# Second block's feed-forwards of a two-block network on one Trainium2 core: later gate/up groups and two down groups as pairs of 64-row matmuls, four outputs to a group

## The reference

```python
def swiglu_2(h, w_gate, w_up, w_down):
    return (jax.nn.silu(h @ w_gate) * (h @ w_up)) @ w_down

# in each layer l of second_block:
#   hdn = swiglu_2(rms_norm(x, norm_pre[l, 0]), ffn1_w_gate[l], ffn1_w_up[l], ffn1_w_down[l])
#   x = x + 0.5 * rms_norm(hdn, norm_post[l, 0])
#   ... the mixer of the layer ...
#   hdn = swiglu_2(rms_norm(x, norm_pre[l, 2]), ffn2_w_gate[l], ffn2_w_up[l], ffn2_w_down[l])
#   x = x + 0.5 * rms_norm(hdn, norm_post[l, 2])
```

## Time and profile before

| what | value |
|---|---|
| time, median of 3 runs | 3773.07 us |
| fastest and slowest of the 3 | 3771.24 and 3773.1 us |
| span of the profiled execution, first to last instruction | 3763.7 us |
| median less that span (launch and end of the program) | 9.4 us |
| PE busy | 3619.1 us, 96% |
| DVE busy | 2059.1 us, 55% |
| ACT busy | 1319.3 us, 35% |

### The profile page before, as it was taken

One profiled execution on the slowest core, in us unless ns is written; L12 is line 12 of the kernel. 1 busy time (PEld: TensorE's weight loads), 2 busy tenths in 40 slices (PEclk: granted clock), 3 DMA queues, 4 the chain that ended last, 5 costly groups with the idle time before them and its releaser, 6 DMA issues.

```text
span 3763.7 us, 51648 instructions
## 1 busy us (share of the span) xinstructions
PE 3619.1 (96%) x21638; PEld 3065.3 (81%) x21638; DVE 2059.1 (55%) x2975; ACT 1319.3 (35%) x1941; POOL 161.8 (4%) x129
## 2 busy tenths in 40 slices
PE   7999999999999899999999999899999999999998
PEld 5866788999978567898988897598888888888887
DVE  4125766755661476476754467674446444566345
ACT  3115344433442344343532233442234223334222
POOL 0000310000000121000000002000000000010000
PEclk9999899999999999999999999999999999999999
DMA  6414011122121131222332222123222222222221
GB/s 265 148 66 157 34 46 68 68 79 90 68 90 56 41 103 57 94 86 91 123 112 101 92 100 73 35 100 108 93 98 101 100 91 100 101 79 102 100 101 56
DMA packets 51381, 345.55 MB, mean 92 GB/s; under 512 B 5792, under 2 KB 8000, under 8 KB 12240
## 3 DMA queue, kind: packets, MB, share of 16 engines
q1 hardware_dynamic: 43632, 305.29, 22.8%
q0 software_dynamic: 5216, 34.88, 2.5%
q10 hardware_dynamic: 2304, 2.10, 0.2%
HBM read 340.14 MB, written 2.10 MB: 91 GB/s over the span
## 4 chain that ended last, share of the span: by engine, by line
PE 84%; DVE 7%; ACT 3%; issue 3%; DMA 2%; POOL 1%; DVEq 0%; ACTq 0%; SPq 0%; POOLq 0%
PE PS L536 38%; PE PS L569 20%; PE PS L2406 8%; PE PS L538 4%; PE PS L1319 2%; PE PS L2278 2%; PE PS L1335 1%; DMA raw<-in_panels 1%; DVE nmax_a L1468 1%; PE PS L1374 1%; ACT WH L508 1%; DVE WL L513 1%; PE PS L1613 1%; PE PS L1906 1%; PE PS L878 1%
## 5 line engine op out<-in xcount | busy, mean ns | idle before, releaser
L513 DVE TENSOR_TENSOR WL<-raw,WH 128x2048 fp32r<-128x2048 f32 x232 | 531.3, 2292 | 276.7 <-ACT WH L508 276.5
L508 ACT ACTIVATE WH<-raw 128x2048 fp32r<-128x2048 f32 x232 | 441.7, 1907 | 439.1 <-PE PS L536 308.9
L536 PE MATMUL PS<-XH_a,WH 128*128 128x512 f32 x448 | 174.3, 389 | 0.0
L536 PE MATMUL PS<-XL_a,WH 128*128 128x512 f32 x448 | 174.3, 389 | 0.0
L536 PE MATMUL PS<-XH_a,WL 128*128 128x512 f32 x448 | 174.3, 389 | 0.0
L536 PE MATMUL PS<-XH_b,WH 128*128 128x512 f32 x448 | 174.3, 389 | 0.0
L536 PE MATMUL PS<-XL_b,WH 128*128 128x512 f32 x448 | 174.3, 389 | 0.0
L536 PE MATMUL PS<-XH_b,WL 128*128 128x512 f32 x448 | 174.3, 389 | 0.0
L569 PE MATMUL PS<-XHq,WH 128*128 128x512 f32 (+1 forms) x448 | 159.1, 355 | 2.6 <-DVE XLq L2942 2.6
L2406 PE MATMUL PS<-XH_ff,SH 128*128 128x384 f32 (+1 forms) x512 | 159.9, 312 | 0.1
L2406 PE MATMUL PS<-XL_ff,SH 128*128 128x384 f32 (+1 forms) x512 | 159.6, 312 | 0.0
(11 more groups left out here) (532 smaller groups left out, 9652.7 us busy)
## 6 DMA issues: line engine op xcount, KB each, us to landing
raw<-in_panels SPq DMA_DIRECT2D x264, 1024.0 KB, 4.8
ada_win<-in_ada_panels POOLq DMA_DIRECT2D x18, 1024.0 KB, 5.1
ada_at<-in_ada_panels SPq DMA_DIRECT2D x14, 1024.0 KB, 4.8
piece<-in_ada_panels SPq DMA_DIRECT2D x20, 512.0 KB, 6.6
ada_start<-in_ada_panels POOLq DMA_DIRECT2D x6, 1024.0 KB, 18.5
FX<-in_dft_x POOLq DMA_DIRECT2D x2, 2048.0 KB, 8.0
X<-in_xT SPq DMA_DIRECT2D x4, 768.0 KB, 11.2
out<-X ACTq DMA_DIRECT2D x16, 128.0 KB, 1.7
```

What stands on the lines that cost most here:

```text
L508: H.up(ac.activation(WH[s].rearrange("p k n -> p (k n)"), raw[:, n % 2, :], ACT.Copy), n)
L513: L.up(ve.tensor_tensor(WL[s].rearrange("p k n -> p (k n)"), raw[:, n % 2, :], WH[s].bitcast(F32).rearrange("p k n -> p (k n)"), ALU.subtr ...
L536: t = te.matmul(PS[:, j, :], lhsT, x[:, k, 0:SEQ], start=st, stop=end)
```

## The change

`te_rows` takes the place of `te_gemm` for `up1`, `up2`, `down0` and `down1` of all four feed-forwards. It takes four outputs (two panels) to a group, in PSUM banks 0 to 3, and goes over them in four steps i. In each step there are two outputs at once, i and o = (i + 2) % 4: one matmul over partitions 0 to 63 into output i's bank, then one over partitions 64 to 127 into output o's bank, and so on through k and the three products. In steps 0 and 1 every output gets one half of its contraction, in steps 2 and 3 the other half. Outputs 0 and 2 (in an up stage: two gates) are complete after step 2, outputs 1 and 3 (the two ups) after step 3. Both panels of a group are waited for at its start and marked as used up at its end. ACT and DVE do the two chunks of a group together: `two_gates` and `two_hidden` on DVE, two `silu` and two `high` on ACT. `SPLITS`, the panels, the slots and the other stages are as they were.

```diff
--- before.py
+++ after.py
@@ -543,6 +543,42 @@
                 if beside:
                     beside(p, 2)
 
+        def te_rows(name, n, nk, XH, XL, ready, evac):
+
+            p0 = FIRST[name]
+
+            def halves(m, to, k, rows, first, last):
+                s, cut = slot_of(p0 + m // 2), slice(m % 2 * P, m % 2 * P + P)
+                for q, (w, x) in enumerate(((WH, XH), (WH, XL), (WL, XH))):
+                    yield (PS[:, to, :], w[s][rows, k, cut], x[rows, k, 0:SEQ],
+                           first and k == 0 and q == 0, last and k == nk - 1 and q == 2)
+
+            for g in range(n // 2):
+                ms = range(4 * g, 4 * g + 4)
+                for m in ms:
+                    te.wait_ge(*L[p0 + m // 2])
+                for i in range(4):
+                    o = (i + 2) % 4
+                    for j in (i, o):
+                        if i < 2:
+                            wait_bank(j)
+                        else:
+                            te.wait_ge(*T[(name, "half", ms[j])])
+                    for k in range(nk):
+                        if g == 0 and i == 0:
+                            ready(k)
+                        for a, b in zip(halves(ms[i], i, k, rows(0), i < 2, i > 1), halves(ms[o], o, k, rows(1), i < 2, i > 1)):
+                            t = te.matmul(*a[:3], start=a[3], stop=a[4])
+                            u = te.matmul(*b[:3], start=b[3], stop=b[4])
+                    for j, done in ((i, t), (o, u)):
+                        if i < 2:
+                            T.up(done, (name, "half", ms[j]))
+                        else:
+                            B.up(done, (name, ms[j]))
+                            evac(ms[j], j)
+                for p in (2 * g, 2 * g + 1):
+                    B.mark(("panel", p0 + p))
+
         def te_first(name, XH, XL, ready, beside, evac):
 
             p0 = FIRST[name]
@@ -3002,10 +3038,10 @@
                 if g == 0:
                     te_wide(up, name, nk, whole(b["XH"]), whole(b["XL"]), evac_up, before, place)
                 else:
-                    te_gemm(up, nk, NC, b["XH"], b["XL"], False, lambda k: None, evac_up)
+                    te_rows(up, nk, NC, b["XH"], b["XL"], lambda k: None, evac_up)
                 ready = lambda k: te.wait_ge(*V[(up, "HL", k)])
                 if g < len(GROUPS[name]) - 1:
-                    te_gemm(down, 4, nk, b["HH"], b["HL"], False, ready, evac_down)
+                    te_rows(down, 4, nk, b["HH"], b["HL"], ready, evac_down)
                 else:
                     te_late(down, nk, whole(b["HH"]), whole(b["HL"]), ready, evac_late, f"{name}.y")
 
@@ -3023,7 +3059,14 @@
                     A.up(ac.activation(b["HH"][:, c, :], gate(c), ACT.Copy), (up, "HH", c))
 
                 def evac_up(m, j):
-                    if g or m >= 4:
+                    if g:
+                        if j:
+                            for c in (m // 2 - 1, m // 2) if m % 4 == 3 else ():
+                                high(c)
+                        elif m % 4 == 0:
+                            silu(m // 2)
+                            silu(m // 2 + 1)
+                    elif m >= 4:
                         (high if j else silu)(m // 2)
                     elif m == 0:
                         for step in (silu, high):
@@ -3039,6 +3082,9 @@
             ve_halve(g3)
             for g, nk in enumerate(GROUPS[name]):
                 up, down = f"{name}.up{g}", f"{name}.down{g}"
+
+                def gate_bank(c):
+                    return 2 * c % 4 if g else place(2 * c)
 
                 def gated(c):
                     ve.wait_ge(*B[(up, 2 * c)])
@@ -3046,7 +3092,7 @@
                         ve.wait_ge(*V[(up, "HL", c - 2)])
                     elif g:
                         ve.wait_ge(*V[(f"{name}.up{g - 1}", "HL", GROUPS[name][g - 1] - 1)])
-                    V.up(ve.tensor_tensor(gate(c), PS[:, place(2 * c) if g == 0 else 0, :], RN[:], ALU.mult),
+                    V.up(ve.tensor_tensor(gate(c), PS[:, gate_bank(c), :], RN[:], ALU.mult),
                          (up, "gated", c))
 
                 def low(c):
@@ -3068,30 +3114,51 @@
                     for c in range(2):
                         low(c)
 
+                def two_gates(c):
+                    for i in (c, c + 1):
+                        gated(i)
+                        ve.wait_ge(*A[(up, "silu", i)])
+                        V.up(ve.tensor_tensor(gate(i), gate(i), RN[:], ALU.mult), (up, "gate", i))
+
+                def two_hidden(c):
+                    for i in (c, c + 1):
+                        ve.wait_ge(*B[(up, 2 * i + 1)])
+                        ve.wait_ge(*V[(up, "gate", i)])
+                        V.up(ve.tensor_tensor(gate(i), PS[:, (2 * i + 1) % 4, :], gate(i),
+                                              ALU.mult), (up, "hidden", i))
+                    for i in (c, c + 1):
+                        low(i)
+
                 def evac_up(m, j):
                     c = m // 2
-                    if g == 0 and m < 4:
+                    if g:
+                        if m % 4 == 0:
+                            two_gates(c)
+                        elif m % 4 == 2:
+                            two_hidden(c - 1)
+                    elif m < 4:
                         if m == 0:
                             first_two()
                             gated(2)
                     elif j == 0:
-                        if g or m > 4:
+                        if m > 4:
                             gated(c)
                         ve.wait_ge(*A[(up, "silu", c)])
                         V.up(ve.tensor_tensor(gate(c), gate(c), RN[:], ALU.mult), (up, "gate", c))
                     else:
                         ve.wait_ge(*B[(up, m)])
                         ve.wait_ge(*V[(up, "gate", c)])
-                        V.up(ve.tensor_tensor(gate(c), PS[:, place(m) if g == 0 else 1, :], gate(c), ALU.mult),
+                        V.up(ve.tensor_tensor(gate(c), PS[:, place(m), :], gate(c), ALU.mult),
                              (up, "hidden", c))
                         low(c)
 
-                def evac_down(m, j):
+                def evac_down(step, j):
+                    m = step + (0, 1, -1, 0)[step % 4]
                     ve.wait_ge(*B[(down, m)])
                     if g == 0:
-                        V.up(ve.tensor_copy(Y[:, m, :], PS[:, j, :]), (down, "x", m))
+                        V.up(ve.tensor_copy(Y[:, m, :], PS[:, m % 4, :]), (down, "x", m))
                     else:
-                        V.up(ve.tensor_tensor(Y[:, m, :], PS[:, j, :], Y[:, m, :], ALU.add), (down, "x", m))
+                        V.up(ve.tensor_tensor(Y[:, m, :], PS[:, m % 4, :], Y[:, m, :], ALU.add), (down, "x", m))
                 ve_gemm(up, nk, evac_up)
                 if g < len(GROUPS[name]) - 1:
                     ve_gemm(down, 4, evac_down)
```

## The result

The changed kernel takes 3829.67 us (median of 4 runs, 3821.21 to 3834.4) against 3772.15 us for the kernel before (4 runs, 3766.14 to 3773.1): a ratio of 1.0149, 95% interval 1.0132 to 1.0166, slower by 57.5 us. The profiled executions have spans of 3819.9 and 3763.7 us, 56.2 us apart. The forecast was 3823 us, and the median lies at the upper end of its own range, 3800 to 3830 us.

A forecast was written before the change was run, and what follows sets the result against it. The prediction took PE, busy 3619 of 3763.7 us, as the bound. Pairs 0, waits 39.6 and clock 10 us gave +50 us on the median of 3773.07: 3823 us, own range 3800 to 3830, whole range 3776 to 3850.

The forecast's parts named there:

- Part 1: 4224 whole-height matmuls in the rewritten stages become pairs, each at the price of one matmul, 0.2266 us: 0 us.
- bounds 113 us apart: Limits for the pairs: streaming alone, 0.2132 us a pair, -56.6 us; a second remainder in every pair, 0.24 us, +56.6 us.
- first rival: Pairs in the rewritten stages reach the streaming rate, 0.213 to 0.216 us each: 3778 to 3799 us, chance 0.20.
- costlier pair: Rival: a pair costs more than one matmul; at 7 ns more 3847 us, at 13 ns about 3870; chance 0.13.
- estimate of 4 ns more a pair: By the skill page, each pair costs 4 ns more than one matmul, the whole 17 us more; not taken into the forecast.
- Part 2: PE waits behind group ends, where the panel split precedes the results on ACT and DVE: 9.9 us a feed-forward, +39.6 us.
- short ones: PE's waits at step 1 of a following `te_rows` group: 0.4 us each, nine a feed-forward, 3.6 us.
- the sum: 0 + 39.6 + 10 = +50 us on the profiled execution, span 3763.7 to 3814.
- long ones: PE's waits for HL chunks, once each a feed-forward: 2.5 us in down1 behind up1, 3.8 us in down2 behind up2.
- Part 3: PE at half clock behind all four 3.8 us pauses and half of the four 2.5 us ones: +10 us, bounds 0 and 14.

The follow-up runs named there:

- e1: Changed kernel, but in the four rewritten stages ACT and DVE do a group's last two outputs ahead of the late panel split: 3769.6 us, ratio 1.0002.
- e5: e1 with the matmuls over partitions 64 to 127 left out but for one of 24 in each step: 3778.67 us in one run.
- e3: Changed kernel with the order of e1 only in the last group of up1 and of up2: 3793.11 us, ratio 1.0062.
- e4: Changed kernel with the order of e1 in all groups but the last of up1 and up2: 3806.53 us, ratio 1.0097.
- e2: Changed kernel's dependencies and ACT and DVE order, but whole-height matmuls of 128 rows instead of pairs: 3822.01 us, ratio 1.0141.
- e7: The changed kernel once more, unaltered, on the same chip as e6: 3824.78 us, ratio 1.0137.
- e6: Changed kernel with spare matmuls ahead of PE's two long waits in each feed-forward, 9 in down1 and 14 in down2: 3821.81 us, ratio 1.0129.

## Why the prediction was right, point by point

**Part 1, the pairs at 0 us.** Right, and the decision between bounds 113 us apart fell the right way: 0.227 us a pair in the trace, ratio 1.0002 in e1. Of its two grounds, the rows of float32 pairs carried over. The other, that each half has to change its weights between its own two matmuls, is borne out only so far: by e5 the 13 ns are there for one half alone, but that the change of weights is what takes them was argued and is not shown. The first rival (streaming rate), the costlier pair and the estimate of 4 ns more a pair by the Trainium skill (TensorE: Matmul & The Clock Gate, Measured speedup vs the span model) are out: the second matmul starts 0.003 to 0.06 us behind the first, but that offset stays as it is and isn't paid again in every pair. The chances did not quite follow from the text: of the first rival's 3778 to 3799 us nearly all lies above 3780.6 us, yet only 0.06 of its 0.20 was counted as slower.

**Part 2, the waits at 39.6 us.** Right in place, number and cause; e3 and e4 take the two kinds away one by one. By the starts on the trace the short ones are 0.44 to 0.47 us (0.4 in the sum), the long ones 2.5 and 3.6 us (2.5 and 3.8): 10.2 us a feed-forward, 41 in all. Inside the chain small errors cancel, which is luck: ACT starts 0.10 us later than worked out, DVE's operations without a wait follow each other by 0.60 us (2087.21 and 2087.81) and not by 0.69, and behind a bank PE restarts 0.15 us after DVE's end (1999.19 and 1999.34) and not 0.06. The one in down2 was put 0.2 us too long because PE gets there late: it asks for chunk 4 at T + 3.02 and not T + 2.72, mostly for the change back to whole height, which the sum held at nothing. In e2, where the height never changes, this wait is 3.8 us.

**Part 3, the clock at +10 us.** The size was right: six stretches at half clock in the profiled execution, as assumed, 1.5 us each (1.7 in the sum), 9 us. That it was just six is luck, since the same kernel had four in e7's. That all four of the longer and half of the shorter pauses would have one was wrong in detail: it was three of four of each. Its share of the whole times is not resolved by e6 and e7; from the trace it is.

**What the sum lacked.** 41 + 9 = 50 us, and the spans are 56 us apart. The rest is 1.7 us a feed-forward: 0.4 us for the changes between whole and half height (e1), for which the prediction held nothing since no row gave their price, and some 1.3 us for the slow first pairs behind eleven restarts (0.30 instead of 0.227 us for the first, a few ns for the next). This second term could have been read from the trace of the kernel before, at a wait ahead of matmuls of 256 columns, whose usual distance is 0.12 us and which here is 0.23:

```profile
3201.51 0.39 PE L569 MATMUL PS<-XHq,WH 128*128 128x256 f32 x1 [1.04 <-DVE XLq L2942]
3201.74 0.28 PE L569 MATMUL PS<-XLq,WH 128*128 128x256 f32 x1
```

The Trainium skill's rule that a change of tiling mode drains the array (TensorEngine Tiling (Array Packing), Key Properties) fits the changes of height: 0.32 us instead of 0.227 at the way in. That it is a drain, and not something else at that place, no run shows.

## What to carry to other kernels

When outputs are grouped, look at what is released only at the group's end and at what stands behind the waiting instruction on the other engines: here a split that had been harmless at the half of a group came ahead of the results that PE wanted, and 4.2 us of it cost 57 us in all. Do the results first and refill the slots after, and the loss is gone. Half-height pairs of the whole contraction were no gain on matmuls that already fill the array: a pair took as long as the whole matmul had, 0.227 us. A choice between two far bounds is best made by the row that shares the most with the new operation (height and columns here, not the type).

## What the runs showed of the hardware that was not expected

- The two halves of the array run side by side at the same pace: once L572 was 0.003, 0.017 or 0.063 us behind L571, it stayed so until the next wait, dozens of pairs, both at 0.2267 us.
- The some 13 ns between the streaming of 512 columns (213 ns, worked out in the prediction from the distances at 256 and 512 columns) and the distance of two matmuls of the rounded type are there for one half alone (e5), for two halves and for the whole array alike. They are also there between the 14 spare matmuls of e6, which all have the same weights but load them anew each time.
- Behind a wait the first matmul is slow: the second one starts 0.335 us after it at whole height (e2) and some 0.30 to 0.31 us at half height, where 0.227 is usual. At a change of height without a wait it is 0.32 us and then 0.335.
- A pause of 2.3 or 3.4 us of idle PE is followed by a stretch at 1.2 GHz in some cases and in others not (six of eight in one execution of the changed kernel, four of eight in another; four and six of eight in e2 and e4); with the pauses filled, none of eight had one. Such a stretch of 3.4 us costs some 1.5 us.
- Two executions of the same instructions ahead of the change ended up to 16.6 us apart, while the stretch behind them repeated to 0.1 us within a kernel, as long as the clock was full. For a change this late in a kernel, the stretch in the trace resolves more than the whole time does.
